# Scattering the experts' results by an exact zero-one matrix, in high and low parts, with the gate applied on VectorE

## The chip, the cores and the metric

One core of a Trainium2 chip. The metric is the device time in microseconds of one launch of the whole program; lower is better.

## The reference

Two stacked blocks over 256 tokens of width 1024. The second layer of the first block ends in a mixture of eight experts, and this is the part that the change touches. Cut to what matters:

```python
logits = (t @ w_router).astype(jnp.float32) + b_router
top_v, top_i = lax.top_k(logits, TOP_K)                     # 2 of 8
top_w = jax.nn.softmax(top_v, -1)
gates = jnp.sum(jax.nn.one_hot(top_i, N_EXPERTS) * top_w[..., None], axis=1)
out = jnp.zeros_like(t)                                     # 256 tokens x 1024
for e in range(N_EXPERTS):                                  # 3584 hidden columns each
    out = out + gates[:, e:e + 1] * _swiglu(t, wg[e], wu[e], wd[e])
x = _layer_norm(DEEPNORM_ALPHA * x + (1.0 + g_f) * out, ln_g, ln_b)
```

## The kernel before, in words

Every large matrix product is made from float32 in three products of a shorter type (fp32r in the profile): a value is split into a high part (ScalarE copies it into the shorter type, `split_hi`, line 430) and a low part (VectorE subtracts the high part from the value, `split_lo`, line 439), and TensorE adds high*high, high*low and low*high (`mm3`, lines 444 to 446). The weights stream from memory in chunks of 128x2048 values, into a ring, and the parts of a chunk lie in one of three buffers `HI` and `LO`. So ScalarE may split chunk j only when TensorE has finished chunk j-3 (`used`), VectorE takes the low part after ScalarE, and TensorE waits for the low part (`lo`).

In the expert stage each expert works on at most 128 tokens, gathered from 256. It has seven steps b (512 hidden columns each); n = 7x + b counts all steps. TensorE's order in step n is: first gate chunk g0, the four transposes of the hidden values of step n-1 (line 544), second gate chunk g1, up chunks u0 and u1, then the two down chunks d0 and d1 of step n-1, which add into PSUM banks 5 and 6 over the seven steps of an expert. Each chunk is 12 matmuls of 512 columns.

An expert's result comes out of the banks while the next expert's step b = 0 has ended on VectorE: `dve_y` (line 2087) multiplies the two banks by a row of gains and writes the float32 tile `YE`. TensorE then scatters it to the tokens in four plain float32 matmuls (`pe_scatter`, line 1908): one after g1 of each of the steps b = 1 to 4, in bank 7, with the stationary matrix `PGT` (for each place the token and its gate). VectorE adds each quarter to `X` (line 1914). `PGT` comes from `PG`, made on VectorE (`dve_select`, lines 1853 and 1854), turned by TensorE (`pe_turn`) and copied by ScalarE (line 1897). The last expert's result is scattered after the loop (`pe_last_scatter`), in four banks, and is followed on TensorE by products of another part (`pe_keys`, line 1636).

The order of the work is written out by hand, and every engine runs its own list in order. ScalarE and VectorE split three chunks ahead of the program's step: at the loop's start g0, g1 and u0 are split. So in step n ScalarE's list is: split u1, copy of the turned hidden values (line 2004), split d0, silu (2031), split d1, split g0 of the next step, split g1, split u0. VectorE's list is: split u1, low part of the hidden values (2009), split d0, scatter's addition or the select, split d1, split g0 of the next step, product of gate and up (2068), split g1, split u0, and, in step b = 0, `dve_y`.

```python
def dve_y(v, x):
    if x > 1:
        v.wait_ge(*pe_moe("scatter", x - 2, 3))
    for nb in range(2):
        ns = slice(512 * nb, 512 * nb + 512)
        v.wait_ge(*(pe_moe("lastdown") if (x, nb) == (7, 0) else used(CH[f"moe{x}d"][13])))
        z = v.tensor_tensor(YE[:, x % 2, ns], PS[:, 5 + nb, :], GB2[:, ns], ALU.mult)
```

Of the kernel before, what the change touches and what calls it, by code (L numbers as in the profile page):

```python
# [7 lines left out]
F32 = mybir.dt.float32  # L8
# [221 lines left out]
def emit_program(nc, ctx, A, out):  # L230
# [1514 lines left out]
    HM = ar(6144, 2, 1024)  # L1745
    RK, RP, RP2, GG, LGT = [ar(8192 + 16 * i, 2, 8) for i in range(5)]
    m1, den2, CNT = ar(8272, 2), ar(8274, 2), ar(8280, 8)
    PP, PG, PGT = ar(8448, 2, 2, 128), ar(8960, 2, 2, 128), ar(9472, 2, 256)
    SGm, HFm = ar(9984, 2, 512), ar(11008, 2, 512)
    YE = ar(12032, 2, 1024)  # L1750
    GB2, LG2, LB2 = ar(14080, 1024), ar(15104, 1024), CST[:, C_DEC:C_DEC + 1024]
    CMP, CM2 = ar(9984, 2, 8, 8), ar(10112, 2, 8, 8)
    SCR, SHR = ar(12032, 1024), ar(13056, 1024)
    GH = X1H[:, :, :].rearrange("p a b -> p (a b)").rearrange("p (s c n) -> p s c n", s=2, c=8)
    GL = X1L[:, :, :].rearrange("p a b -> p (a b)").rearrange("p (s c n) -> p s c n", s=2, c=8)
    RHm = X2H[:, :, :].rearrange("p a b -> p (a b)").rearrange("p (s c n) -> p s c n", s=4, c=4)
    RLm = X2L[:, :, :].rearrange("p a b -> p (a b)").rearrange("p (s c n) -> p s c n", s=4, c=4)

    def pe_router(t):
        t.wait_ge(*act_two("memory", "router"))  # L1760
# [87 lines left out]
    def dve_select(v, x):  # L1848
        s_ = x % 2
        if x > 1:  # L1850
            v.wait_ge(*pe_moe("turn", x - 2))
        for k in range(2):
            v.tensor_scalar(PP[:, s_, k, :], iota, RP[:, k, x:x + 1], None, ALU.is_equal)
            z = v.tensor_scalar(PG[:, s_, k, :], iota, RP[:, k, x:x + 1], GG[:, k, x:x + 1], ALU.is_equal, ALU.mult)
        z.then_inc(*dve_moe.up("select", x))

    def gather_bank(x, half):
# [28 lines left out]
                        gh.bitcast(F32), ALU.subtract).then_inc(*dve_moe.up("gather", x, half))  # L1886

    def pe_turn(t, x):
        if x:
            t.wait_ge(*dve_moe("gather", x, 1))  # L1890
        turn(t, [(PS[:, 7 if x else 6, 128 * k:128 * k + 128], PG[:, x % 2, k, :]) for k in range(2)]).then_inc(*pe_moe.up("turn", x))

    def act_turn(a, x):
        a.wait_ge(*pe_moe("turn", x))
        if x > 1:
            a.wait_ge(*pe_moe("scatter", x - 2, 3))
        a.activation(PGT[:, x % 2, :], PS[:, 7 if x else 6, 0:256], ACT.Copy).then_inc(*act_moe.up("turn", x))
# [4 lines left out]
    def pe_scatter(t, x, q):  # L1902
        k, ns = q // 2, slice(512 * (q % 2), 512 * (q % 2) + 512)
        if q == 0:
            t.wait_ge(*dve_moe("y", x))
        if x < 7:
            t.wait_ge(*(dve_moe("scatter", x, q - 1) if q else act_moe("turn", x + 1)))
        t.matmul(PS[:, scatter_bank(x, q), :], PGT[:, x % 2, 128 * k:128 * k + 128], YE[:, x % 2, ns], start=True,  # L1908
                 stop=True).then_inc(*pe_moe.up("scatter", x, q))

    def dve_scatter(v, x, q):
        k, ns = q // 2, slice(512 * (q % 2), 512 * (q % 2) + 512)
        v.wait_ge(*pe_moe("scatter", x, q))
        v.tensor_tensor(X[:, k, ns], X[:, k, ns], PS[:, scatter_bank(x, q), :], ALU.add).then_inc(
            *dve_moe.up("scatter", x, q))

    def pe_between(t, x, b, after):
        if x > 0 and 1 <= b <= 4 and after == "g":  # L1920
            pe_scatter(t, x - 1, b - 1)
        if x < 7 and (b, after) == (5, "u"):
            pe_gather(t, x + 1, 0)
        if x < 7 and (b, after) == (6, "g"):
            pe_gather(t, x + 1, 1)
        if x < 7 and (b, after) == (6, "u"):
            pe_turn(t, x + 1)

    def act_between(a, x, b, after):
        if x < 7 and (b, after) == (5, "u"):  # L1930
            act_gather(a, x + 1, 0)
        if x < 7 and (b, after) == (6, "g"):
            act_gather(a, x + 1, 1)
        if x < 7 and (b, after) == (6, "u"):
            act_turn(a, x + 1)

    def dve_between(v, x, b, after):
        if x > 0 and 1 <= b <= 4 and after == "g":
# [8 lines left out]
    def pe_moe_program(t):  # L1947
        pe_router(t)
        pe_gather(t, 0, 0)
        pe_gather(t, 0, 1)  # L1950
        pe_turn(t, 0)
        for n in range(7 * NEXP + 1):
            x, b = n // 7, n % 7
            for q, nm in ((0, "g"), (1, "u")) if x < NEXP else ():
                bk = 2 * q + n % 2
                for k in range(2):
                    i = CH[f"moe{x}{nm}"][2 * b + k]
                    t.wait_ge(*lo(i))
# [12 lines left out]
            if n > 0:
                pe_down(t, n - 1)

    def pe_down(t, n):
        x, b = n // 7, n % 7
        for half in range(2):
            i = CH[f"moe{x}d"][2 * b + half]
            t.wait_ge(*lo(i))
            if half == 0:
                t.wait_ge(*dve_moe("hidlo", n))  # L1980
            if x > 0 and b == 0 and half == 0:
                t.wait_ge(*dve_moe("y", x - 1))
            for nb, c in ((0, 0), (0, 1), (1, 0), (1, 1)):
                ns, q = slice(512 * nb, 512 * nb + 512), 2 * half + c
                z = mm3(t, PS[:, 5 + nb, :], RHm[:, n % 3, q, :], RLm[:, n % 3, q, :], hi_of(i)[:, c, ns],
                        lo_of(i)[:, c, ns], b == 0 and q == 0, b == 6 and q == 3)
                if n == 55 and half == 1 and (nb, c) == (0, 1):
                    z.then_inc(*pe_moe.up("lastdown"))
            z.then_inc(*used.up(i))
            if n == 54 and half == 0:  # L1990
                pe_turn_hidden(t, 55)
# [7 lines left out]

    def act_hidden_moe(a, n):  # L2000
        a.wait_ge(*pe_moe("hid", n))
        if n > 2:
            a.wait_ge(*used(CH[f"moe{(n - 3) // 7}d"][2 * ((n - 3) % 7) + 1]))
        a.activation(RHm[:, n % 3], PS[:, 4, :].rearrange("p (c n) -> p c n", c=4), ACT.Copy).then_inc(
            *act_moe.up("hid", n))

    def dve_hidden_moe(v, n):
        v.wait_ge(*act_moe("hid", n))
        v.tensor_tensor(RLm[:, n % 3], PS[:, 4, :].rearrange("p (c n) -> p c n", c=4), RHm[:, n % 3].bitcast(F32),
                        ALU.subtract).then_inc(*dve_moe.up("hidlo", n))  # L2010

    def act_moe_program(a):
# [3 lines left out]
        split_hi(a)  # L2016
        act_gather(a, 0, 0)
        act_gather(a, 0, 1)
        act_turn(a, 0)
        for n in range(7 * NEXP + 1):  # L2020
            x, b = n // 7, n % 7
            if x < NEXP:
# [56 lines left out]

    def dve_y(v, x):  # L2080

        if x > 1:
            v.wait_ge(*pe_moe("scatter", x - 2, 3))
        for nb in range(2):
            ns = slice(512 * nb, 512 * nb + 512)
            v.wait_ge(*(pe_moe("lastdown") if (x, nb) == (7, 0) else used(CH[f"moe{x}d"][13])))
            z = v.tensor_tensor(YE[:, x % 2, ns], PS[:, 5 + nb, :], GB2[:, ns], ALU.mult)
        z.then_inc(*dve_moe.up("y", x))


    def pe_last_scatter(t):
# [34 lines left out]

    XG, HT2 = ar(0, 8, 128), ar(1024, 4, 128)
    WB2 = [ar(2048, 2048), ar(4096, 2048)]
    P1, G1, GT1, Y1 = ar(8448, 2, 128), ar(8704, 2, 128), ar(8960, 256), ar(12032, 1024)
    H1 = ar(9984, 512)  # L2130

    def wb(i, c):
# [1069 lines left out]

    def vector_y(v):
        dve_y(v, 7)

    count = Count()
    for program in (sync_program, scalar_program, vector_program, gpsimd_program, tensor_program, vector_y, sp_rest,
                    act_rest_body, dve_rest_body, pe_rest_body, sync_program2, scalar_program2, vector_program2,
                    gpsimd_program2, tensor_program2):
        program(count)  # L3210
# [9 lines left out]
    with nc.Block() as blk:  # L3220
# [6 lines left out]
            tensor_program2(t)  # L3227

        def scalar_end(a):
            with a.If(more(a)):  # L3230
                act_rest_body(a)
            scalar_program2(a)

# [46 lines left out]
```

## Time and profile before

| | |
|---|---|
| three runs | 2753.72, 2753.80, 2757.09 us |
| median | 2753.8 us |
| span of the profiled execution | 2756.4 us (no other time of it is given) |
| TensorE busy in it | 2655.7 us, 96% |
| VectorE | 2194.9 us, 80% |
| ScalarE | 1519.4 us, 55% |
| GpSimd | 47.4 us, 2% |
| mean granted TensorE clock | 0.973 of full speed |
| expert stage, from its first chunk to its last | 597.4 to 1591.4 us |

Times in the rows count from the span's start. A matmul's time is from its start to its modelled end, and matmuls overlap, so what one costs is the distance between two starts, which the chain of waits gives. PE is TensorE, PEld its weight loads, DVE VectorE, ACT ScalarE, POOL GpSimd. Names such as `PS<-AR` are the tiles written and read: PS is PSUM, AR the arena in which most tiles of this stage lie.

### The profile page before, as it was taken

Reading aid. Unit: us, or ns where it says so; the run is one execution under the profiler, and the core shown is the slowest. Engines: PE = TensorE matmul, PEld = TensorE weight load, DVE = VectorE, ACT = ScalarE, POOL = GpSimd, SP = SyncE. Lnnn points to the kernel's source line nnn. Section 1 sums busy time; section 2 is a strip of 40 time slices with the busy share of each in tenths; the row PEclk is TensorE's granted clock in tenths of the full one; section 3 lists DMA queues with packets and bytes.
Section 4 is the critical chain, followed back from the end, with each engine's and each line's share of the span. In section 5 each row is a group of like instructions: output and inputs, shape, how many; then the busy total and the mean of one; then the engine's idle time right before and its main releaser. Section 6 shows DMA issues by size and latency. Waiting matters only on the chain.

```text
span 2756.4 us, 37885 instructions
## 1 busy us (share of the span) xinstructions
PE 2655.7 (96%) x15712; PEld 2358.6 (86%) x15712; DVE 2194.9 (80%) x2513; ACT 1519.4 (55%) x1567; POOL 47.4 (2%) x83
## 2 busy tenths in 40 slices
PE   6969999989999999999999999999999999999998
PEld 5859998878888888888888889999899999998898
DVE  6967677778888888888888879885487788954777
ACT  3514335547677677777777754544554564444554
POOL 2000000000000000000000000000000000000000
PEclk9979999989999999999999999999999998999999
DMA  8649865369999999999999952354455533444453
GB/s 312 235 162 336 312 240 168 120 212 378 351 350 353 345 359 349 360 348 358 348 359 346 364 184 87 135 183 173 157 184 184 186 125 130 154 153 168 153 184 115
DMA packets 376065, 669.86 MB, mean 243 GB/s; under 512 B 26825, under 2 KB 199503, under 8 KB 371023
## 3 DMA queue, kind: packets, MB, share of 16 engines
q1 hardware_dynamic: 358400, 662.55, 68.2%
q10 hardware_dynamic: 17487, 4.83, 0.7%
q8 instruction: 126, 2.06, 0.3%
q14 instruction: 52, 0.43, 0.0%
HBM read 663.13 MB, written 4.19 MB: 242 GB/s over the span
## 4 chain that ended last, share of the span: by engine, by line
PE 88%; DVE 7%; ACT 2%; DMA 1%; issue 1%; POOL 0%; ACTq 0%; SPq 0%; DVEq 0%; POOLq 0%
PE PS L444 25%; PE PS L446 24%; PE PS L445 24%; PE PS L544 2%; PE PS L2477 2%; DVE LO L439 2%; PE PS L1636 2%; DVE AR L2767 1%; PE PS L1871 1%; PE PS L1908 1%; PE PS L2363 1%; DMA RAW<-in_w_ada_dram 1%; ACT HI L430 1%; DVE AR L697 1%; PE PS L2354 1%
## 5 line engine op out<-in xcount | busy, mean ns | idle before, releaser
L439 DVE TENSOR_TENSOR LO<-RAW,HI 128x2048 fp32r<-128x2048 f32 x410 | 930.2, 2273 | 231.5 <-ACT HI L430 231.3
L430 ACT ACTIVATE HI<-RAW 128x2048 fp32r<-128x2048 f32 x410 | 780.0, 1903 | 346.3 <-PE PS L446 292.9
L444 PE MATMUL PS<-X1H,HI 128*128 128x256 f32 (+1 forms) x2128 | 611.4, 287 | 6.2 <-DVE X1L L584 4.2
L445 PE MATMUL PS<-X1L,HI 128*128 128x256 f32 (+1 forms) x2128 | 605.5, 285 | 0.0
L446 PE MATMUL PS<-X1H,LO 128*128 128x256 f32 (+1 forms) x2128 | 605.2, 284 | 0.0
L444 PE MATMUL PS<-HI,X1H 128*128 128x512 f32 x1056 | 431.6, 409 | 0.9 <-DVE LO L439 0.4
L444 PEld LDWEIGHTS PS<-X1H,HI 128*128 128x128 f32 (+1 forms) x2128 | 409.4, 192 | 11.1 <-issue 8.5
L446 PE MATMUL PS<-HI,X1L 128*128 128x512 f32 x1056 | 413.7, 392 | 0.0
L445 PE MATMUL PS<-LO,X1H 128*128 128x512 f32 x1056 | 413.0, 391 | 0.0
L445 PEld LDWEIGHTS PS<-X1L,HI 128*128 128x128 f32 (+1 forms) x2128 | 409.6, 192 | 2.0
L446 PEld LDWEIGHTS PS<-X1H,LO 128*128 128x128 f32 (+1 forms) x2128 | 409.3, 192 | 0.8
L439 DVE TENSOR_TENSOR LO<-AR,HI 128x2048 fp32r<-128x2048 f32 (+1 forms) x147 | 334.8, 2278 | 58.6 <-ACT HI L430 57.7
L430 ACT ACTIVATE HI<-AR 128x2048 fp32r<-128x2048 f32 (+1 forms) x147 | 280.2, 1907 | 121.3 <-PE PS L446 117.0
L444 PE MATMUL PS<-HI,X2H 128*128 128x512 f32 x840 | 333.9, 398 | 3.3 <-DVE LO L439 3.3
L445 PE MATMUL PS<-LO,X2H 128*128 128x512 f32 x840 | 330.8, 394 | 0.0
L446 PE MATMUL PS<-HI,X2L 128*128 128x512 f32 x840 | 330.5, 393 | 0.0
L444 PEld LDWEIGHTS PS<-HI,X1H 128*128 128x128 f32 x1056 | 199.2, 189 | 48.3 <-issue 8.5
L445 PEld LDWEIGHTS PS<-LO,X1H 128*128 128x128 f32 x1056 | 199.4, 189 | 45.5 <-issue 6.7
L446 PEld LDWEIGHTS PS<-HI,X1L 128*128 128x128 f32 x1056 | 198.8, 188 | 42.9
L2767 DVE SCALAR_TENSOR_TENSOR AR<-AR,PC 128x256 f32<-128x256 f32 x480 | 193.9, 477 | 0.1
L444 PEld LDWEIGHTS PS<-HI,X2H 128*128 128x128 f32 x840 | 160.4, 191 | 35.7 <-DVE LO L439 3.7
L446 PEld LDWEIGHTS PS<-HI,X2L 128*128 128x128 f32 x840 | 159.8, 190 | 34.1
(392 smaller groups left out, 2869.0 us busy)
## 6 DMA issues: line engine op xcount, KB each, us to landing
RAW<-in_w_in_dram SPq DMA_DIRECT2D x66, 1024.0 KB, 5.2
RAW<-in_expert_w_gate_dram SPq DMA_DIRECT2D x66, 1024.0 KB, 5.2
RAW<-in_expert_w_up_dram SPq DMA_DIRECT2D x64, 1024.0 KB, 5.2
RAW<-in_expert_w_down_dram SPq DMA_DIRECT2D x62, 1024.0 KB, 5.3
RAW<-in_ffn_w_up_dram SPq DMA_DIRECT2D x55, 1024.0 KB, 5.6
AR<-in_expert_w_down_dram SPq DMA_DIRECT2D x50, 1024.0 KB, 5.3
AR<-in_expert_w_up_dram SPq DMA_DIRECT2D x48, 1024.0 KB, 5.5
AR<-in_expert_w_gate_dram SPq DMA_DIRECT2D x46, 1024.0 KB, 5.2
```

Of the source, the lines that this page charges most:

```text
L430: a.activation(HI[:, n % NH, 0:size(i)], raw_at(i), ACT.Copy).then_inc(*hi.up(i))
L439: v.tensor_tensor(LO[:, m % NH, 0:n], raw_at(i), HI[:, m % NH, 0:n].bitcast(F32), ALU.subtract).then_inc(*lo.up(i))
L444: t.matmul(o, lh, rh, start=first, stop=False)
L445: t.matmul(o, lh, rl, start=False, stop=False)
L446: return t.matmul(o, ll, rh, start=False, stop=last)
L544: z = t.transpose(d, s_, ident[0:n, 0:n])
L697: v.scalar_tensor_tensor(o, slot, pcol("c", k), o, ALU.mult, ALU.add).then_inc(*dve_ada.up("step", m))
L1636: z = t.matmul(PS[:, bank, 256 * nb:256 * nb + 256], w[:, c, 128 * nb:128 * nb + 128], cols[:, c, :], start=(c == 0), stop=(c == 7))
L1871: z = t.matmul(PS[:, gather_bank(x, half), 128 * c:128 * c + 128], HM[:, k, 512 * half + 128 * c:512 * half + 128 * c + 128], PP[:, x % 2, ...
L1908: t.matmul(PS[:, scatter_bank(x, q), :], PGT[:, x % 2, 128 * k:128 * k + 128], YE[:, x % 2, ns], start=True, stop=True).then_inc(*pe_moe.u ...
L2477: z = t.matmul(PS[:, b, 256 * k:256 * k + 256], MF[:, c, 128 * k:128 * k + 128], w[:, c, :], start=(c == 0), stop=(c == 7))
L2767: v.scalar_tensor_tensor(UC[:, c, :], UP[:, c, k:k + 256], pcol(f"cv_dw_w{l}", 8 * k + c), UC[:, c, :], ALU.mult, ALU.add).then_inc(*dve_t ...
```

## The change

The select now makes only the zero-one matrix `PP`, which is turned itself (for expert x instead of x+1, in the same place of the order; that of expert 7 is new there, and that of expert 0 ahead of the loop is gone) and copied into a tile `PPT` of its own. `YE` is split like a weight chunk: ScalarE copies it into `YH` (`act_y`), VectorE subtracts (`dve_y_lo`) into `YL`. The scatter is two fp32r matmuls a quarter. VectorE's addition multiplies by the gate. `YE`, `PPT`, `YH` and `YL` are single; the hidden values' parts have two buffers instead of three. The diff, cut:

```diff
-    YE = ar(12032, 2, 1024)
+    YE = ar(12032, 1024)
-    RHm = X2H[:, :, :].rearrange("p a b -> p (a b)").rearrange("p (s c n) -> p s c n", s=4, c=4)
+    RHm = X2H[:, 0:4, :].rearrange("p a b -> p (a b)").rearrange("p (s c n) -> p s c n", s=2, c=4)
+    YH, YL = [t_[:, 4:8, :].rearrange("p a b -> p (a b)") for t_ in (X2H, X2L)]
...
         for k in range(2):
-            v.tensor_scalar(PP[:, s_, k, :], iota, RP[:, k, x:x + 1], None, ALU.is_equal)
-            z = v.tensor_scalar(PG[:, s_, k, :], iota, RP[:, k, x:x + 1], GG[:, k, x:x + 1], ALU.is_equal, ALU.mult)
+            z = v.tensor_scalar(PP[:, s_, k, :], iota, RP[:, k, x:x + 1], None, ALU.is_equal)
...
     def pe_turn(t, x):
-        if x:
-            t.wait_ge(*dve_moe("gather", x, 1))
-        turn(t, [(PS[:, 7 if x else 6, 128 * k:128 * k + 128], PG[:, x % 2, k, :]) for k in range(2)]).then_inc(*pe_moe.up("turn", x))
+        t.wait_ge(*(dve_moe("gather", x + 1, 1) if x < 7 else dve_moe("scatter", 6, 3)))
+        turn(t, [(PS[:, 7, 128 * k:128 * k + 128], PP[:, x % 2, k, :]) for k in range(2)]).then_inc(*pe_moe.up("turn", x))
...
         if q == 0:
-            t.wait_ge(*dve_moe("y", x))
-        if x < 7:
-            t.wait_ge(*(dve_moe("scatter", x, q - 1) if q else act_moe("turn", x + 1)))
-        t.matmul(PS[:, scatter_bank(x, q), :], PGT[:, x % 2, 128 * k:128 * k + 128], YE[:, x % 2, ns], start=True,
-                 stop=True).then_inc(*pe_moe.up("scatter", x, q))
+            t.wait_ge(*dve_moe("ylo", x))
+            t.wait_ge(*act_moe("turn", x))
+        elif x < 7:
+            t.wait_ge(*dve_moe("scatter", x, q - 1))
+        places = PPT[:, 128 * k:128 * k + 128]
+        t.matmul(PS[:, scatter_bank(x, q), :], places, YH[:, ns], start=True, stop=False)
+        t.matmul(PS[:, scatter_bank(x, q), :], places, YL[:, ns], start=False, stop=True).then_inc(
+            *pe_moe.up("scatter", x, q))
...
-        v.tensor_tensor(X[:, k, ns], X[:, k, ns], PS[:, scatter_bank(x, q), :], ALU.add).then_inc(
-            *dve_moe.up("scatter", x, q))
+        v.scalar_tensor_tensor(X[:, k, ns], PS[:, scatter_bank(x, q), :], GG[:, k, x:x + 1], X[:, k, ns], ALU.mult,
+                               ALU.add).then_inc(*dve_moe.up("scatter", x, q))
...
     def act_hidden_moe(a, n):
         a.wait_ge(*pe_moe("hid", n))
-        if n > 2:
-            a.wait_ge(*used(CH[f"moe{(n - 3) // 7}d"][2 * ((n - 3) % 7) + 1]))
+        if n > 1:
+            a.wait_ge(*used(CH[f"moe{(n - 2) // 7}d"][2 * ((n - 2) % 7) + 1]))
...
             if 0 < n < 56:                                     # act_moe_program, end of step n
                 split_hi(a)
                 split_hi(a)
+                if b == 0:
+                    act_y(a, x - 1)
...
             if x < NEXP:                                       # dve_moe_program, start of step n
                 split_lo(v)
+                if x > 0 and b == 1:
+                    dve_y_lo(v, x - 1)
...
+    def act_y(a, x):
+        a.wait_ge(*dve_moe("y", x))
+        a.activation(YH, YE, ACT.Copy).then_inc(*act_moe.up("yhi", x))
+
+    def dve_y_lo(v, x):
+        v.wait_ge(*act_moe("yhi", x))
+        v.tensor_tensor(YL, YE, YH.bitcast(F32), ALU.subtract).then_inc(*dve_moe.up("ylo", x))
```

For the last expert `act_y` runs on ScalarE and `dve_y_lo` on VectorE at the start of the block that follows the loop, ahead of `pe_last_scatter`.

## Rows read from the trace of the kernel before

**Rows 1.** the page: busy shares, and the granted clock (tenths) in 40 slices

```profile
PE 2655.7 (96%) x15712; PEld 2358.6 (86%) x15712; DVE 2194.9 (80%) x2513; ACT 1519.4 (55%) x1567; POOL 47.4 (2%) x83
...
PEclk9979999989999999999999999999999998999999
```

**Rows 2.** busy us (and instructions) in the expert stage, one stretch per expert; PEclk is granted clock

```profile
core 0: us, PE busy (x) PEld busy (x) DVE busy (x) ACT busy (x) POOL busy (x), PEclk, DMA share, GB/s
...
722.00:846.00 124.00, 124.00 (x571) 101.68 (x570) 108.83 (x68) 87.56 (x58) 0.00 (x0) 1.00 0.97 352
```

**Rows 3.** chain of waits in the stage, start and us of each link, in order

```profile
735.96 0.23 PE PS L446
736.19 0.86 PE PS L1908 x2
```

**Rows 4.** TensorE in order of time, around expert 0's first scatter

```profile
736.03 1.02 PE L1908 MATMUL PS<-AR 128*128 128x512 f32 x2
```

**Rows 5.** VectorE in order of time, at the same border

```profile
732.32 2.29 DVE L439 TENSOR_TENSOR LO<-AR,HI 128x2048 fp32r<-128x2048 f32 x1 [0.34 <-ACT HI L430]
734.53 1.28 DVE L2087 TENSOR_TENSOR AR<-PS,AR 128x512 f32<-128x512 f32 x2
735.73 2.28 DVE L439 TENSOR_TENSOR LO<-RAW,HI 128x2048 fp32r<-128x2048 f32 x1
...
740.73 0.68 DVE L1914 TENSOR_TENSOR X<-X,PS 128x512 f32<-128x512 f32 x1
```

**Rows 6.** ScalarE in order of time, at the same border

```profile
730.37 1.92 ACT L430 ACTIVATE HI<-AR 128x2048 fp32r<-128x2048 f32 x1 [0.80 <-PE PS L446]
733.09 1.92 ACT L430 ACTIVATE HI<-RAW 128x2048 fp32r<-128x2048 f32 x1 [0.80 <-PE PS L446]
```

**Rows 7.** groups of instructions by line and shape, ScalarE: count, busy us, mean ns

```profile
L430 ACT ACTIVATE HI<-RAW 128x1024 fp32r<-128x1024 f32 x4 | 4.2, 1050 | 0.0
```

**Rows 8.** the same for VectorE

```profile
L439 DVE TENSOR_TENSOR LO<-RAW,HI 128x1024 fp32r<-128x1024 f32 x4 | 4.9, 1223 | 1.5 <-ACT HI L430 1.5
...
L2112 DVE SCALAR_TENSOR_TENSOR X<-X,SM,AR 128x512 f32<-128x512 f32 x4 | 2.8, 750 | 0.1
```

**Rows 9.** two TensorE gaps elsewhere, in stretches (columns as rows 2)

```profile
168.50:171.80 3.30, 0.06 (x1) 0.00 (x0) 3.08 (x2) 0.00 (x0) 0.00 (x0) 1.00 0.72 217
...
172.90:176.30 3.40, 3.40 (x10) 2.62 (x9) 1.78 (x2) 0.00 (x0) 0.00 (x0) 0.50 0.49 161
...
2552.00:2555.40 3.40, 0.03 (x1) 0.00 (x0) 1.31 (x3) 2.12 (x8) 1.03 (x3) 1.00 0.92 305
...
2556.40:2562.20 5.80, 5.74 (x27) 5.74 (x28) 4.24 (x11) 4.54 (x9) 0.11 (x1) 0.50 0.00 0
```

**Rows 10.** chain of waits at the stage's end

```profile
1591.39 0.70 DVE AR L2087
...
1592.37 3.70 PE PS L1908 x8
1596.08 6.92 PE PS L1636 x32
```

**Rows 11.** ScalarE's work just ahead of it

```profile
1587.84 3.29 ACT L1624 ACTIVATE RAW<-RAW,PC 128x256 f32<-128x256 f32 x8
```

**Rows 12.** VectorE in order of time, the first select

```profile
590.13 0.28 DVE L1853 TENSOR_SCALAR AR<-CST,AR 128x128 f32<-128x128 f32 x1
590.33 0.34 DVE L1854 TENSOR_SCALAR AR<-CST,AR 128x128 f32<-128x128 f32 x1
...
590.78 0.34 DVE L1854 TENSOR_SCALAR AR<-CST,AR 128x128 f32<-128x128 f32 x1
```

**Rows 13.** TensorE ahead of the stage's first chunk, in order of time

```profile
591.17 6.21 PE L1871 MATMUL PS<-AR 128*128 128x128 f32 x32 [2.85 <-DVE AR L1854]
597.22 0.38 PE L544 MATMUL PS<-CST,AR 128*128 128x128 f32 x2
597.36 0.48 PE L444 MATMUL PS<-HI,X1H 128*128 128x512 f32 x1
```

More of the change, by code:

```diff
@@ L252, in emit_program @@
     WR = sb("WR", [128, 8, 8])
+    PPT = sb("PPT", [128, 256], F32R)
     PS = ctx.enter_context(nc.psum_tensor("PS", [128, 8, 512], F32))
@@ L1747, in emit_program @@
     m1, den2, CNT = ar(8272, 2), ar(8274, 2), ar(8280, 8)
-    PP, PG, PGT = ar(8448, 2, 2, 128), ar(8960, 2, 2, 128), ar(9472, 2, 256)
+    PP = ar(8448, 2, 2, 128)
     SGm, HFm = ar(9984, 2, 512), ar(11008, 2, 512)
-    YE = ar(12032, 2, 1024)
+    YE = ar(12032, 1024)
     GB2, LG2, LB2 = ar(14080, 1024), ar(15104, 1024), CST[:, C_DEC:C_DEC + 1024]
@@ L1755, in emit_program @@
     GL = X1L[:, :, :].rearrange("p a b -> p (a b)").rearrange("p (s c n) -> p s c n", s=2, c=8)
-    RHm = X2H[:, :, :].rearrange("p a b -> p (a b)").rearrange("p (s c n) -> p s c n", s=4, c=4)
-    RLm = X2L[:, :, :].rearrange("p a b -> p (a b)").rearrange("p (s c n) -> p s c n", s=4, c=4)
+    RHm = X2H[:, 0:4, :].rearrange("p a b -> p (a b)").rearrange("p (s c n) -> p s c n", s=2, c=4)
+    RLm = X2L[:, 0:4, :].rearrange("p a b -> p (a b)").rearrange("p (s c n) -> p s c n", s=2, c=4)
+    YH, YL = [t_[:, 4:8, :].rearrange("p a b -> p (a b)") for t_ in (X2H, X2L)]
     def pe_router(t):
@@ L1888, in pe_turn @@
     def pe_turn(t, x):
-        if x:
-            t.wait_ge(*dve_moe("gather", x, 1))
-        turn(t, [(PS[:, 7 if x else 6, 128 * k:128 * k + 128], PG[:, x % 2, k, :]) for k in range(2)]).then_inc(*pe_moe.up("turn", x))
+        t.wait_ge(*(dve_moe("gather", x + 1, 1) if x < 7 else dve_moe("scatter", 6, 3)))
+        turn(t, [(PS[:, 7, 128 * k:128 * k + 128], PP[:, x % 2, k, :]) for k in range(2)]).then_inc(*pe_moe.up("turn", x))
     def act_turn(a, x):
         a.wait_ge(*pe_moe("turn", x))
-        if x > 1:
-            a.wait_ge(*pe_moe("scatter", x - 2, 3))
-        a.activation(PGT[:, x % 2, :], PS[:, 7 if x else 6, 0:256], ACT.Copy).then_inc(*act_moe.up("turn", x))
+        if x > 0:
+            a.wait_ge(*pe_moe("scatter", x - 1, 3))
+        a.activation(PPT[:, :], PS[:, 7, 0:256], ACT.Copy).then_inc(*act_moe.up("turn", x))
     def scatter_bank(x, q):
@@ L1925, in pe_between @@
             pe_gather(t, x + 1, 1)
-        if x < 7 and (b, after) == (6, "u"):
-            pe_turn(t, x + 1)
+        if (b, after) == (6, "u"):
+            pe_turn(t, x)
     def act_between(a, x, b, after):
@@ L1933, in act_between @@
             act_gather(a, x + 1, 1)
-        if x < 7 and (b, after) == (6, "u"):
-            act_turn(a, x + 1)
+        if (b, after) == (6, "u"):
+            act_turn(a, x)
     def dve_between(v, x, b, after):
@@ L1950, in pe_moe_program @@
         pe_gather(t, 0, 1)
-        pe_turn(t, 0)
         for n in range(7 * NEXP + 1):
@@ L1984, in pe_down @@
                 ns, q = slice(512 * nb, 512 * nb + 512), 2 * half + c
-                z = mm3(t, PS[:, 5 + nb, :], RHm[:, n % 3, q, :], RLm[:, n % 3, q, :], hi_of(i)[:, c, ns],
+                z = mm3(t, PS[:, 5 + nb, :], RHm[:, n % 2, q, :], RLm[:, n % 2, q, :], hi_of(i)[:, c, ns],
                         lo_of(i)[:, c, ns], b == 0 and q == 0, b == 6 and q == 3)
@@ L2001, in act_hidden_moe @@
         a.wait_ge(*pe_moe("hid", n))
-        if n > 2:
-            a.wait_ge(*used(CH[f"moe{(n - 3) // 7}d"][2 * ((n - 3) % 7) + 1]))
-        a.activation(RHm[:, n % 3], PS[:, 4, :].rearrange("p (c n) -> p c n", c=4), ACT.Copy).then_inc(
+        if n > 1:
+            a.wait_ge(*used(CH[f"moe{(n - 2) // 7}d"][2 * ((n - 2) % 7) + 1]))
+        a.activation(RHm[:, n % 2], PS[:, 4, :].rearrange("p (c n) -> p c n", c=4), ACT.Copy).then_inc(
             *act_moe.up("hid", n))
@@ L2008, in dve_hidden_moe @@
         v.wait_ge(*act_moe("hid", n))
-        v.tensor_tensor(RLm[:, n % 3], PS[:, 4, :].rearrange("p (c n) -> p c n", c=4), RHm[:, n % 3].bitcast(F32),
+        v.tensor_tensor(RLm[:, n % 2], PS[:, 4, :].rearrange("p (c n) -> p c n", c=4), RHm[:, n % 2].bitcast(F32),
                         ALU.subtract).then_inc(*dve_moe.up("hidlo", n))
@@ L2018, in act_moe_program @@
         act_gather(a, 0, 1)
-        act_turn(a, 0)
         for n in range(7 * NEXP + 1):
@@ L2080, in dve_y @@
     def dve_y(v, x):
-        if x > 1:
-            v.wait_ge(*pe_moe("scatter", x - 2, 3))
+        if x > 0:
+            v.wait_ge(*pe_moe("scatter", x - 1, 3))
         for nb in range(2):
@@ L2086, in dve_y @@
             v.wait_ge(*(pe_moe("lastdown") if (x, nb) == (7, 0) else used(CH[f"moe{x}d"][13])))
-            z = v.tensor_tensor(YE[:, x % 2, ns], PS[:, 5 + nb, :], GB2[:, ns], ALU.mult)
+            z = v.tensor_tensor(YE[:, ns], PS[:, 5 + nb, :], GB2[:, ns], ALU.mult)
         z.then_inc(*dve_moe.up("y", x))
+    def act_y(a, x):
[4 more added lines that the diff above has]
+        v.tensor_tensor(YL, YE, YH.bitcast(F32), ALU.subtract).then_inc(*dve_moe.up("ylo", x))
     def pe_last_scatter(t):
@@ L2128, in emit_program @@
     WB2 = [ar(2048, 2048), ar(4096, 2048)]
-    P1, G1, GT1, Y1 = ar(8448, 2, 128), ar(8704, 2, 128), ar(8960, 256), ar(12032, 1024)
+    P1, G1, GT1, Y1 = ar(8448, 2, 128), ar(8704, 2, 128), ar(8960, 256), ar(11008, 1024)
     H1 = ar(9984, 512)
@@ L3204, in vector_y, with scalar_y @@
         dve_y(v, 7)
+        dve_y_lo(v, 7)
+    def scalar_y(a):
+        act_y(a, 7)
     count = Count()
-    for program in (sync_program, scalar_program, vector_program, gpsimd_program, tensor_program, vector_y, sp_rest,
+    for program in (sync_program, scalar_program, vector_program, gpsimd_program, tensor_program, vector_y, scalar_y, sp_rest,
                     act_rest_body, dve_rest_body, pe_rest_body, sync_program2, scalar_program2, vector_program2,
@@ L3229, in scalar_end @@
         def scalar_end(a):
-            with a.If(more(a)):
+            flag = more(a)
+            scalar_y(a)
+            with a.If(flag):
                 act_rest_body(a)
```

## The prediction

> **What bounds the kernel now.** The page comes first [rows 1]: TensorE is busy for 96% of the span, at full granted clock nearly throughout. The stage that the change touches lies at 597 to 1591 us, and the stretches by expert show what it is bound by [rows 2]: in the 124.00 us of one expert TensorE is busy for 124.00, at clock 1.00, with VectorE at 108.8 and ScalarE at 87.6. So a matmul removed there is time removed, and a wait of TensorE put there is time added, one for one. The chain of waits in the stage [rows 3] is TensorE alone and gives true prices: an fp32r matmul of 512 columns is 0.23 us (twelve of them, a chunk, 2.72 us by the starts of the chunks), and one float32 quarter of the scatter, which runs as two passes, is 0.86 us. The next thing to see is how little room the scatter has. At the border between experts 0 and 1 TensorE begins it at 736.03 [rows 4], while VectorE ends `YE` at 734.53 + 1.28 = 735.81 [rows 5]: 0.22 us ahead. The other borders that I looked at are the same to 0.01 us. `YE` can't come sooner as the lists stand: it stands behind the low part of u0 (732.32), which began when ScalarE's high part ended (730.37 + 1.92), which began when TensorE gave the buffer free [rows 5, 6].
>
> **The change, part by part.** All against the profiled execution, whose span of 2756.4 us lies 2.6 above the median of 2753.8; I carry the differences to the median, since the work is the same.
>
> *The matmuls of the scatter.* In the loop seven experts have four quarters: 28 times 0.86 become 28 times 2 x 0.227 (0.454), so 28 x 0.41 = 11.4 us go [rows 3]. All on the path.
>
> *The split of the result, and who waits.* This is the large term, so I replay one border on the lists. `YE` is ready at 735.81. ScalarE has done its high part of u0 at 732.29 and now stands at `act_y`, as the next entry of its list is behind it. It starts at 735.85. A high part of 128x1024 takes 1.05 us [rows 7]: to 736.90. Only then comes the high part of u1, which before ran at 733.09 [rows 6]; now it runs from 736.81 (ScalarE's operations overlap by 0.09) to 738.73. VectorE's list has the low part of u1 ahead of `dve_y_lo`: before at 735.73, now 738.76, and the next operation starts 2.21 later, at 740.97. The low part of 128x1024 takes 1.22 us [rows 8]: to 742.19. TensorE's scatter, due at 736.03, waits for it until 742.24, so 6.2 us, and since TensorE runs its list in order, u0 (whose parts have long been ready) stands behind it, and every later chunk with it. In the meantime the others get ahead: u1 is ready at 741.0, and d0 follows at about 745.0 against its need at 748, so nothing is late next. Buffers of the hidden values: two are enough, since the products that used a buffer are on TensorE's list ahead of the transposes that refill it: 0 us. 7 borders x 6.2 = 43.4 us. Bounds: if u1's split were not late, `YE`'s two parts would still take 1.05 + 1.22, so at least 2.1 us a border (14.7); if ScalarE's copy took as long as a full one (1.92, rows 6), 7.1 us (49.7). The rows of just these shapes decide for 6.2.
>
> *The clock after the wait.* No gap of 6 us is in this stage, but elsewhere gaps show what follows [rows 9]. After a gap of 3.3 us the granted clock was 0.50 (the lower level, 1.2 GHz) for 3.4 us of work. After one of 4.4 us it was 0.50 in the 5.8 us of work that followed. At the lower level work takes twice as long, so half of that is lost: 1.7 or 2.9 us. For the low end I set 0, as gaps of 1 us at the end of this stage cost nothing. I take 1.7 for each of the seven, the nearer end because the longer the gap, the more of the slow stretch falls into the gap itself: 11.9 us, bounds 0 and 20.3. The Trainium skill ("TensorE: Matmul & The Clock Gate", on HAM oscillation) says that repeated waits of TensorE make its array fall back to the slow clock each time; by that rule each border pays, and the rows above say the same, with the sizes used here. Were the rule not to hold in this stage, the sum would be 11.9 us less.
>
> *VectorE and ScalarE otherwise.* The select loses two of four operations and `dve_y_lo` is one more; in the stage VectorE idles 15 us an expert [rows 2], and ahead of the select's next split it waits for ScalarE anyway: 0. The addition with the gate is a three-operand form: 0.75 against 0.68 us [rows 8, 5], hidden by the same idle time; if that cover were gone, 28 x 0.07 = 2 us. ScalarE's copy of the turned matrix is where it was: 0.
>
> *The front.* The gather waits for the first select [rows 13], whose four operations start at 590.13, 590.33, then the other pair, the last at 590.78 and 0.34 long [rows 12]. With two left it ends 0.5 us sooner. The two transposes ahead of the loop go (597.22 to 597.36, 0.14). Together -0.6 us. Expert 7's two transposes are new inside the loop, for the same 0.14: +0.1.
>
> *The end.* Before: second half of `YE` 1591.39 to 1592.09, scatter at 1592.37, next products at 1595.91 to 1596.08 [rows 10]. After: ScalarE is free by 1591.13 [rows 11], so 1592.13 + 1.05 + 1.22 and the 0.28 to TensorE, that is 1594.7, or 1594.9 if ScalarE too needs 0.28 in the new block. Eight fp32r matmuls take 1.8 (the eight float32 passes took 3.6), so the next products start at 1596.6, +0.7 us. VectorE's chain of norms starts 2.0 later, but ScalarE's squares, which need it, come late enough behind TensorE's products to take up nearly all of it: 0, at most 1.2 (both are covered by the bounds). TensorE's gap of 3.5 us is like the 3.3 in [rows 9]: +1.7. Together +2.4, bounds 0.6 and 3.6.
>
> **Sum:** -11.4 + 43.4 + 11.9 - 0.6 + 0.1 + 2.4 = +45.8 us. 2753.8 + 45.8 = 2799.6, said as 2800.
>
> **The rivals.**
> 1. *The split comes in time, and only the matmuls count* (faster). The place is the wait of the first quarter: with the two parts of the result ready within 0.2 us, 28 x 0.41 and the front are gained, -11.9, and the end gives back 2.4: 2744. It decides from a loss of 1.4 us a border on ((11.4 + 0.6 - 0.1 - 2.4) / 7); below that the kernel is faster. For it: ScalarE is busy for only 71% of an expert. Against: the lists; its free time lies elsewhere than where the copy stands, and even with no list in the way 1.05 + 1.22 us don't fit in 0.2. Chance 0.04.
> 2. *The waits come, the clock stays up.* 2800 - 11.9 - 1.7 = 2786. For it: the page's row of the clock is at 9 tenths or full in nearly all slices, though there are waits in many [rows 1]. Against: [rows 9], where the clock fell after both gaps. Chance 0.12.
> 3. *Every gap costs like the longer row, or the scatter in parts saves nothing* (if the program were to run it in the passes of before). The first: 2800 + 7 x 1.2 + 1.2 = 2810; the second: 2800 + 11.4 = 2811. For the first: 6.2 us is nearer to 4.4 than to 3.3. Against the second: operands of this type run at 0.23 us in [rows 3]. Chance 0.2.
> 4. *The wait is shorter*, with 2 to 5 us a border, by something in the lists that I misread: 2753.8 + 7 x 3.5 - 11.4 + 7 x 0.85 + 2.4 = 2775. Chance 0.06.
>
> **How the numbers follow.** The forecast itself has 0.58. A measurement of this kernel tells about 0.2% (5.5 us) from no change. Slower by more than that are the forecast, rivals 2, 3 and 4: 0.94 with a little off for what I haven't seen; faster is rival 1. The range runs from 2783, just under rival 2, to 2814, over both forms of rival 3; rivals 1 and 4 and some unknown are outside.
>
> **What would show it.** In the changed trace TensorE's first scatter matmul of each of seven experts has idle time of about 6 us ahead of it, released by VectorE's subtraction of 128x1024; ScalarE idles 3.5 us ahead of the 128x1024 copy; u1's low part starts 3 us later than before against `YE`. The clock in the stage's slices is no longer 1.00, with half-rate stretches behind each of the gaps. Scatter matmuls stand 0.23 us apart. TensorE's share in an expert falls below 96%. I am wrong if the gap is missing or below 2 us, or if the low half is ready when TensorE comes.

## The result, and the profile after

The changed kernel takes 2806.2 us (median of four runs, 2805.47 to 2809.61) against 2753.76 for the kernel before on the same chip: a ratio of 1.019, with a 95% interval of 1.0177 to 1.0204. It is slower by 52.4 us. The profiled execution took 2806.1 us, with a span of 2804.3.

The page, to be read beside [rows 1]: TensorE does the same number of matmuls, but its share is 95%, and in the row of the clock one slice more reads 8. That one lies behind the stage; the stage's own slices of 70 us still read 9 tenths or more, so the clock has to be looked at closer, below.

```profile
PE 2661.3 (95%) x15712; PEld 2369.8 (85%) x15712; DVE 2204.0 (79%) x2505; ACT 1526.3 (54%) x1575; POOL 47.4 (2%) x83
...
PEclk9979999989999999999999999899999998999999
```

TensorE's list at the first border, in order of time. It answers to [rows 4]: the wait of the first scatter matmul is new, and the matmuls behind it (L445 is the first of each chunk's triples) stand 1.28 us apart in threes, not 0.68.

```profile
731.67 0.39 PE L445 MATMUL PS<-HI,X1H 128*128 128x512 f32 x1
...
738.54 0.80 PE L1910 MATMUL PS<-X2H,PPT 128*128 128x512 f32 x1 [6.03 <-DVE X2L L2101]
739.14 0.63 PE L1911 MATMUL PS<-X2L,PPT 128*128 128x512 f32 x1
739.57 0.63 PE L445 MATMUL PS<-HI,X1H 128*128 128x512 f32 x1
...
740.85 0.63 PE L445 MATMUL PS<-HI,X1H 128*128 128x512 f32 x1
...
742.12 0.63 PE L445 MATMUL PS<-HI,X1H 128*128 128x512 f32 x1
...
743.32 0.39 PE L445 MATMUL PS<-HI,X1H 128*128 128x512 f32 x1
...
744.02 0.39 PE L445 MATMUL PS<-HI,X1H 128*128 128x512 f32 x1
```

VectorE's and then ScalarE's list at the same place, answering to [rows 5, 6].

```profile
728.65 2.29 DVE L440 TENSOR_TENSOR LO<-AR,HI 128x2048 fp32r<-128x2048 f32 x1 [0.35 <-ACT HI L431]
730.86 1.28 DVE L2092 TENSOR_TENSOR AR<-PS,AR 128x512 f32<-128x512 f32 x2
735.06 2.29 DVE L440 TENSOR_TENSOR LO<-RAW,HI 128x2048 fp32r<-128x2048 f32 x1 [2.92 <-ACT HI L431]
737.27 1.22 DVE L2101 TENSOR_TENSOR X2L<-AR,X2H 128x1024 fp32r<-128x1024 f32 x1
```

```profile
732.17 1.06 ACT L2097 ACTIVATE X2H<-AR 128x1024 fp32r<-128x1024 f32 x1 [3.56 <-DVE AR L2092]
733.14 1.89 ACT L431 ACTIVATE HI<-RAW 128x2048 fp32r<-128x2048 f32 x1
```

The reader is to see a chain with no free moment in it: result ready at 730.86 + 1.28 = 732.14, copy of 1.06 us from 732.17 (ScalarE had waited 3.56 us for it), u1's high part at 733.14, its low part at 735.06 (VectorE had waited 2.92 us), the result's low part at 737.27 to 738.49, scatter at 738.54. TensorE idled for 6.03 us. The seven borders are alike: 6.03 or 6.04 us each.

The same places by stretches (columns: length, then busy us and instructions of TensorE, its weight loads, VectorE, ScalarE and GpSimd, then the granted clock). Each pair is a gap and what follows it, at the first three borders; the last line is what follows the 3.13 us gap at the stage's end.

```profile
732.50:738.50 6.00, 0.01 (x1) 0.00 (x0) 3.44 (x3) 5.30 (x5) 0.00 (x0) 0.82 0.57 197
738.50:743.20 4.70, 4.66 (x11) 3.69 (x12) 3.45 (x3) 0.00 (x0) 0.00 (x0) 0.50 0.79 241
...
864.50:870.50 6.00, 0.01 (x1) 0.00 (x0) 3.44 (x3) 5.29 (x5) 0.00 (x0) 0.92 0.58 201
870.50:876.30 5.80, 5.76 (x14) 4.51 (x15) 3.44 (x3) 0.00 (x0) 0.00 (x0) 0.50 0.82 269
996.90:1003.00 6.10, 0.09 (x1) 0.00 (x0) 3.46 (x3) 5.38 (x5) 0.00 (x0) 0.69 0.58 203
1003.00:1006.00 3.00, 2.97 (x7) 2.39 (x8) 3.00 (x3) 0.00 (x0) 0.00 (x0) 0.50 0.93 328
...
1639.00:1643.00 4.00, 4.00 (x18) 3.40 (x19) 3.11 (x6) 0.00 (x0) 0.06 (x1) 1.00 0.06 18
```

The lower level (1.2 GHz) is granted for 4.7, 5.8 and 3.0 us of work here, and over the seven borders for 32.3 us. A matmul is started every 0.43 us there and every 0.23 us at the upper level, so about half of that time is lost, 16.2 us. At the stage's end it is not granted in this execution.

### The profile page after: what moved, and what is told of

The parts are those of the page before. It is cut to its first block, busy times and chain, and to the rows that moved or that the text cites. A ratio compares the mean times of both kernels' runs of the same rounds, so it can differ in the third digit from the quotient of the medians.

```text
span 2804.3 us, 37889 instructions
## 1 busy us (share of the span) xinstructions
PE 2661.3 (95%) x15712; PEld 2369.8 (85%) x15712; DVE 2204.0 (79%) x2505; ACT 1526.3 (54%) x1575; POOL 47.4 (2%) x83
## 4 chain that ended last, share of the span: by engine, by line
PE 87%; DVE 8%; ACT 2%; DMA 2%; issue 1%; POOL 0%; ACTq 0%; SPq 0%; DVEq 0%; POOLq 0%
PE PS L445 25%; PE PS L446 24%; PE PS L447 24%; PE PS L545 2%; DVE LO L440 2%; PE PS L2490 2%; PE PS L1637 1%; ACT HI L431 1%; DVE AR L2780 1%; PE PS L1872 1%; PE PS L2376 1%; DMA RAW<-in_w_ada_dram 1%; PE PS L2367 1%; DVE AR L698 1%; PE PS L726 1%
## 5 line engine op out<-in xcount | busy, mean ns | idle before, releaser
L445 PE MATMUL PS<-X1H,HI 128*128 128x256 f32 (+1 forms) x2128 | 611.4, 287 | 6.0 <-DVE X1L L585 4.2
L445 PE MATMUL PS<-HI,X1H 128*128 128x512 f32 x1056 | 425.4, 403 | 0.9 <-DVE LO L440 0.4
L445 PEld LDWEIGHTS PS<-X1H,HI 128*128 128x128 f32 (+1 forms) x2128 | 409.8, 193 | 10.8 <-issue 8.3
L445 PE MATMUL PS<-HI,X2H 128*128 128x512 f32 x840 | 333.0, 396 | 2.7 <-DVE LO L440 2.7
L445 PEld LDWEIGHTS PS<-HI,X1H 128*128 128x128 f32 x1056 | 202.6, 192 | 44.4 <-issue 1.8
L445 PEld LDWEIGHTS PS<-HI,X2H 128*128 128x128 f32 x840 | 159.9, 190 | 35.0 <-DVE LO L440 3.1
```

What stands on the lines that cost most here:

```text
L445: t.matmul(o, lh, rh, start=first, stop=False)
```

## The experiments

Each was compared with runs of the kernel before on its own chip, whose median was 2755.7 us for e1 to e4 and 2757.3 for e6 to e8; so ratios, not bare times, are compared between groups. There is also a finer measure, which leaves out everything around the stage: the period of an expert, from one run of 16 gather matmuls (at the end of a step b = 6) to the next, taken over six experts of the profiled execution.

**e1, the scatter one step later.** The split stays where the change has it.

```diff
-        if x > 0 and 1 <= b <= 4 and after == "g":
-            pe_scatter(t, x - 1, b - 1)
+        if x > 0 and 2 <= b <= 5 and after == "g":
+            pe_scatter(t, x - 1, b - 2)
```

and the same for VectorE's additions.

> The changed kernel with its four scatter quarters one step later (steps 2 to 5 of the next expert, on TensorE and VectorE); the split of the result stays where it is. Theory A (a wait made by the order of the lists): the 6.03 us wait ahead of the scatter goes, but the high part of u1 still stands behind the copy of the result on ScalarE, so TensorE waits about 2.2 us a border for u1's low part (ready at 741.0 on the clock of the kernel before, wanted at 738.75). 2806.2 - 7 x 3.8 = 2779 if the clock still falls after each of these shorter gaps, 2763 if it doesn't. Theory B (ScalarE and VectorE are short of time for the added copy and subtraction, whatever their place): the same work, so within 5 us of 2806.

Measured: 2771.42 us, ratio 1.0055 (1.004 to 1.007). TensorE's waits in the stage, first the list, then two stretches after gaps:

```profile
PE PS L445 <- DVE LO L440: 18.0, 10, 2.2
```

```profile
740.11 0.50 PE L445 MATMUL PS<-HI,X1H 128*128 128x512 f32 x1 [2.19 <-DVE LO L440]
...
744.04 0.50 PE L445 MATMUL PS<-HI,X2H 128*128 128x512 f32 x1 [0.92 <-DVE LO L440]
```

```profile
740.10:744.00 3.90, 3.01 (x12) 2.18 (x12) 3.90 (x4) 2.98 (x3) 0.00 (x0) 1.00 0.73 237
...
868.80:872.20 3.40, 3.40 (x9) 2.47 (x8) 3.40 (x3) 1.24 (x2) 0.00 (x0) 0.50 0.72 286
```

The wait for the result's parts is gone, and the second one that the first had hidden stands in the open: u1's low part comes 2.19 us late, as expected. After the first such gap the clock stayed up (and a second gap of 0.92 us followed); after the second it fell for 3.4 us. It fell after four of the seven, and the gap of 0.9 us came only behind the three after which it stayed up. So the time lies between the two that theory A gave (2763 and 2779), and theory B, by which the place doesn't matter, is out.

**e2, the split where the engines are free.** Same instructions, other places on the lists: ScalarE copies the result after u1's high part and the copy of the hidden values, VectorE subtracts after d0's low part, and TensorE scatters after u1 instead of after g1.

```diff
-        if x > 0 and 1 <= b <= 4 and after == "g":
+        if x > 0 and 1 <= b <= 4 and after == "u":
             pe_scatter(t, x - 1, b - 1)
...
-        if x > 0 and 1 <= b <= 4 and after == "g":
+        if x > 0 and b == 1 and after == "g":
+            dve_y_lo(v, x - 1)
+        if x > 0 and 1 <= b <= 4 and after == "u":
             dve_scatter(v, x - 1, b - 1)
...
             if 0 < n < 56:
                 act_hidden_moe(a, n - 1)
+                if x > 0 and b == 1:
+                    act_y(a, x - 1)
...
                 split_hi(a)
                 split_hi(a)
-                if b == 0:
-                    act_y(a, x - 1)
...
                 split_lo(v)
-                if x > 0 and b == 1:
-                    dve_y_lo(v, x - 1)
```

> The same instructions as the changed kernel in another order: ScalarE copies the result after u1's high part and the copy of the hidden values, VectorE subtracts after d0's low part, TensorE scatters after u1 of the steps 1 to 4 instead of after g1. Theory A: no wait of TensorE at the borders, granted clock 1.00 through the stage; what is left is the gain on the matmuls, 28 x 0.41 = 11.4 us, and about +0.5 at the end: 2743, faster than both kernels. Theory B: the waits move but stay, total above 2780.

Measured: 2751.97 us (12 runs, 2744.57 to 2756.21), ratio 0.9985 (0.9975 to 0.9995). The waits moved and shrank to a tenth, but were not gone:

```profile
735.00 0.39 PE L447 MATMUL PS<-HI,X1L 128*128 128x512 f32 x1
735.99 0.50 PE L1910 MATMUL PS<-X2H,PPT 128*128 128x512 f32 x1 [0.60 <-DVE X2L L2101]
736.33 0.39 PE L1911 MATMUL PS<-X2L,PPT 128*128 128x512 f32 x1
```

```profile
732.51 2.29 DVE L440 TENSOR_TENSOR LO<-RAW,HI 128x2048 fp32r<-128x2048 f32 x1
734.72 1.22 DVE L2101 TENSOR_TENSOR X2L<-AR,X2H 128x1024 fp32r<-128x1024 f32 x1
```

I had put the subtraction behind d0's low part (732.51), which ends late, and TensorE came 0.6 us too soon; from start to start that is 0.99 instead of 0.23, so 0.76 x 7 = 5.3 us. The clock stayed at 1.00 through the stage. So the same copy and subtraction that made TensorE wait 6.2 us a border in one place cost 0.8 in another, though here the scatter stands 2.7 us later too. Against the 11 us expected the gain is 4.1 by the ratio (1.4 to 6.9), and the stage of the profiled execution is 4.7 us shorter than before; the seven waits are most of what is missing.

**e3, matmuls in the wait.**

```diff
         if q == 0:
+            t.wait_ge(*act_moe("turn", x))
+            if x < 7:
+                for r in range(24):
+                    t.matmul(PS[:, 7, :], GH[:, (x + 1) % 2, r % 8, :], GL[:, (x + 1) % 2, 0:4, :], start=True, stop=True)
             t.wait_ge(*dve_moe("ylo", x))
-            t.wait_ge(*act_moe("turn", x))
```

> The changed kernel with 24 added fp32r matmuls of 512 columns (24 x 0.227 = 5.4 us, on tiles that are ready, into bank 7 ahead of the scatter, which writes over them) in each of the seven waits. The wait itself is thereby kept, only TensorE is busy in it. Theory A (16 us of the loss are the half-rate stretches behind the gaps): clock 1.00 through the stage, 2806.2 - 16.2 = 2790. Rival C (the slow stretches are covered by waits for ScalarE and VectorE, or would be there anyway): 2806, within 3 us.

Measured: 2790.16 us, ratio 1.0122 (1.0108 to 1.0137), against 1.019 of the changed kernel. 168 matmuls more, and 16 us less by the medians, 19 by the ratios.

```profile
732.23 5.60 PE L1908 MATMUL PS<-X1L,X1H 128*128 128x512 f32 x24
738.43 0.50 PE L1913 MATMUL PS<-X2H,PPT 128*128 128x512 f32 x1 [0.60 <-DVE X2L L2104]
...
739.00 0.40 PE L445 MATMUL PS<-HI,X1H 128*128 128x512 f32 x1
...
739.69 0.39 PE L445 MATMUL PS<-HI,X1H 128*128 128x512 f32 x1
```

```profile
600.00:1570.00 970.00, 965.79 (x4464) 799.58 (x4463) 828.69 (x498) 672.66 (x452) 0.00 (x0) 1.00 0.95 343
```

The wait itself is as long as ever (from 732.23 to 738.43), but behind it the triples stand 0.69 us apart at once, and the granted clock of the stage is 1.00. In the profiled executions the stage, from its first gather matmul to the last chunk's end, takes 1048.3 us in the changed kernel and 1033.3 here. So 15.1 of the 16.2 us that I put down to the clock went with it; about 1 us isn't accounted for. The total alone would not say this so closely, since parts outside the stage differ too: at the stage's end the clock fell here, which it had not in the changed kernel, and that piece took 3.7 us longer.

**e4, the gate alone.** The result is not split, so copy and subtraction are gone; one float32 matmul a quarter.

```diff
-    PPT = sb("PPT", [128, 256], F32R)
+    PPT = sb("PPT", [128, 256])
...
-            t.wait_ge(*dve_moe("ylo", x))
+            t.wait_ge(*dve_moe("y", x))
...
-        t.matmul(PS[:, scatter_bank(x, q), :], places, YH[:, ns], start=True, stop=False)
-        t.matmul(PS[:, scatter_bank(x, q), :], places, YL[:, ns], start=False, stop=True).then_inc(
+        t.matmul(PS[:, scatter_bank(x, q), :], places, YE[:, ns], start=True, stop=True).then_inc(
```

> Only one part of the change: the zero-one matrix, turned late and copied as float32, one float32 matmul a quarter, the gate applied in VectorE's addition; the result is not split (no copy, no subtraction), single result tile, two buffers of hidden values. Theory A (the split alone costs): 2753.8 - 0.5, so the kernel before within 2 us. Rival D (a part of the loss comes from the three-operand addition, the single tiles or the two buffers): above 2756, up to 2760.

Measured: 2752.87 us (11 runs), ratio 0.9995 (0.9984 to 1.0006): no change. The gate in the addition, the single tiles, the two buffers and the later turn cost nothing that can be told; the interval leaves room for 1.7 us. The stage took 1000.0 us, against 1000.2 before.

**e6, split as in e2, scatter as in e1.** It takes e2's split and puts the quarters after g1 of steps 2 to 5; these lines are against e2.

```diff
-        if x > 0 and 1 <= b <= 4 and after == "u":
-            pe_scatter(t, x - 1, b - 1)
+        if x > 0 and 2 <= b <= 5 and after == "g":
+            pe_scatter(t, x - 1, b - 2)
```

> e2 with the scatter's quarters after g1 of steps 2 to 5 instead of after u1 of steps 1 to 4, so 2.7 us later against the split. In e2 TensorE still waited 0.76 us a border for the low part. Theory A: those seven waits go (-5.3 us against e2), nothing in the stage is waited for, and the stage is shorter than before by the matmuls, about 11 us; the total is 9 to 12 us under the kernel before of the same chip. Rival (e2 missed its expected gain for another reason, such as dearer chunks beside the added work): the same total as e2, 4 us under the kernel before.

Measured: 2746.96 us, ratio 0.9966 (0.9953 to 0.998), so 9 to 10 us under the kernel before (5 to 13 by the interval), where 9 to 12 were expected. In the stage no scatter matmul waits. One small wait stays, of weight loads for a low part (d1's, at each border), so the stage is 8.5 us shorter than before, and not 11:

```profile
PEld PS L445 <- DVE LO L440: 3.9, 8, 0.5
```

e6 and e1 are the clean pair for the place of the split: the instructions are the same and the scatter stands in the same place, only copy and subtraction have moved. The ratio falls from 1.0055 to 0.9966, and the stage from 1016.9 to 991.6 us.

**e7, the last result by halves.** For the last expert copy, subtraction and the first two quarters' waits go by 512 columns. This is ScalarE's part of the edit, on top of e6:

```diff
+        if x == 7:
+            a.wait_ge(*dve_moe("yfirst"))
+            a.activation(YH[:, 0:512], YE[:, 0:512], ACT.Copy).then_inc(*act_moe.up("yhifirst"))
+            a.wait_ge(*dve_moe("y", x))
+            a.activation(YH[:, 512:1024], YE[:, 512:1024], ACT.Copy).then_inc(*act_moe.up("yhi", x))
+            return
```

> e6 with the last expert's result split by halves of 512 columns, so that TensorE's first quarter after the loop waits for half of the copy and half of the subtraction. The gap of TensorE there, 3.13 us in the changed kernel, falls by about 1.3 us to 1.8, and so does the time against e6: 1 to 1.5 us less. If the end isn't bound by this chain, nothing changes.

Measured: 2744.8 us, ratio 0.9958 (0.9943 to 0.9974). Against e6 that is 2.2 us less, but the two intervals overlap, so by the totals alone it isn't shown. The lists at the stage's end show it, e6 first, then e7:

```profile
1578.92 0.80 PE L1910 MATMUL PS<-X2H,PPT 128*128 128x512 f32 x1 [3.13 <-DVE X2L L2101]
...
1597.33 1.94 PE L545 MATMUL PS<-CST,AR 128*128 128x128 f32 x16 [1.04 <-DVE AR L2311]
```

```profile
1582.34 0.50 PE L1913 MATMUL PS<-X2H,PPT 128*128 128x512 f32 x1 [1.38 <-ACT X2H L2105]
...
1599.65 1.94 PE L545 MATMUL PS<-CST,AR 128*128 128x128 f32 x16 [1.04 <-DVE AR L2328]
```

The gap is 1.38 instead of 3.13 us, a little better than the 1.8 expected. (The profile names ScalarE's second copy as what ended it; the program waits there for VectorE's first half, which ended at 1582.29.) From the scatter to the next transposes it is 17.3 instead of 18.4; in e6 the clock fell after the gap and in e7 it did not. Of the versions that add both parts this one has the lowest median, and it is faster than both kernels.

**e8, the matmuls by themselves.** VectorE writes the result in the shorter type at once, and both matmuls of a quarter use it: the low part is left out and the high part is added twice. The sums that it makes are not the reference's; it is there for its time alone.

```diff
-            z = v.tensor_tensor(YE[:, ns], PS[:, 5 + nb, :], GB2[:, ns], ALU.mult)
+            z = v.tensor_tensor(YH[:, ns], PS[:, 5 + nb, :], GB2[:, ns], ALU.mult)
...
-        t.matmul(PS[:, scatter_bank(x, q), :], places, YL[:, ns], start=False, stop=True).then_inc(
+        t.matmul(PS[:, scatter_bank(x, q), :], places, YH[:, ns], start=False, stop=True).then_inc(
```

> The price of the matmuls by themselves: VectorE writes the result straight in the shorter type and both matmuls of a quarter use it (the low part is left out, and the high part is added twice), so there is no copy, no subtraction and no wait for them. Theory A: 28 x 0.41 = 11.4 us in the loop and 1.5 at the end less than before, no gap at the borders: 2741 against 2753.8. If the shorter type saves nothing in this place: 2753.

Measured: 2742.23 us, ratio 0.9942 (0.9923 to 0.9962), 15.1 us less, where 12.8 were expected; in the profiled executions the stage is 11.1 us shorter and its end 1.5. The period of an expert is the cleanest measure. Here is the first of them in the kernel before, e8 and e6, in this order (one line is the run at the end of expert 0, the next that of expert 1):

```profile
700.36 1.95 PE L1871 MATMUL PS<-AR 128*128 128x128 f32 x16
```

```profile
825.48 1.95 PE L1871 MATMUL PS<-AR 128*128 128x128 f32 x16
```

```profile
697.72 1.95 PE L1872 MATMUL PS<-AR 128*128 128x128 f32 x16
```

```profile
821.24 1.95 PE L1872 MATMUL PS<-AR 128*128 128x128 f32 x16
```

```profile
692.91 1.95 PE L1872 MATMUL PS<-AR 128*128 128x128 f32 x16
```

```profile
816.85 1.95 PE L1872 MATMUL PS<-AR 128*128 128x128 f32 x16
```

That is 125.12, 123.52 and 123.94 us. Taken over six periods it is 125.12, 123.51 and 123.92: the matmuls save 1.61 us an expert, four times 0.40, and e6 gives 0.4 of it back by the small wait above. The changed kernel's period is 131.93 us and e2's 124.37. So against e8, which has no split, copy and subtraction cost 8.4 us a border where the change puts them, 0.9 in e2 and 0.4 in e6.

## Why the prediction was right, and where a term was off

*The direction and the total.* +52.4 against +45.8 forecast, 2806.2 within 2783 to 2814. The total alone would speak for the third rival as well (2810 or 2811); it is the rows and the experiments that decide. And it is in part luck that it came so near: the clock at the borders was put 4.3 us too low and the end 1.9 too high.

*The rivals.* The first (split in time) and the fourth (a wait of 2 to 5 us) fell with the gap of 6.03 us, the second with the clock at the borders; the third's price for the clock, 2.9 us each, was too high as mine was too low, and its other form fell with e8's saving.

*The wait.* The replay gave a scatter at 742.24 when it was due at 736.03, 6.2 us. Measured from the end of the last matmul the gap is 6.03, and from the time at which the scatter was due 6.2. Each link is as worked out: ScalarE's copy 1.06 (1.05), its wait for it 3.56 (3.5), low part 1.22. e1 shows both halves of the argument, and e6 against e1 that the place of the split makes the wait, and not the work in it.

*The matmuls.* 11.4 us forecast for seven experts; e8 gives 7 x 1.61 = 11.3. At the stage's end, where the clock stayed up, the scatter's matmuls stand 0.23 us apart, as forecast.

*The clock.* This is the mis-sized term. I took 1.7 us a border, on the ground that a longer gap hides more of the slow stretch. The rows at the borders show 4.67, 5.79, 3.01, 4.92, 5.92, 3.06 and 4.95 us of work at the lower level, so 2.3 us each, 16.2 in all and not 11.9. The argument was wrong in one point: the longer gap also brought a slow stretch of 6.83 us at all seven, twice the 3.4 that followed the 3.3 us gap of [rows 9], so more was left of it. The other gap of [rows 9], of 4.4 us, already had 5.8 us of slow work behind it, more than the shorter one and not less. e3 confirms the size but for 1 us. The Trainium skill ("TensorE: Matmul & The Clock Gate", on HAM oscillation) tells of a kernel whose repeated waits of about 3 to 5 us drop the array to its slow clock each time; seven of seven gaps of 6.03 us agree with it. e1's gaps of 2.2 us are shorter than those waits, and there the clock still fell at four of seven.

*The front.* The wait of the first gather fell from 2.85 to 2.35 us, the 0.5 forecast. The 0.1 for the two transposes is not seen: from the first gather matmul to the first chunk it is 6.19 us before and 6.21 after.

*The end.* Forecast +2.4, of which 1.7 was the clock. From the last chunk's end to the next part's transposes the profiled execution took 19.57 us before (1591.35 to 1610.92) and 20.11 after (1635.85 to 1655.96): +0.5, near the 0.7 without the clock. In e6 the clock did fall there, and the piece took 21.5 us.

*The gate, the buffers, the select:* 0 forecast, and e4 measures none.

*What the sum leaves open.* Stage: 43.3 (seven waits of 6.19, start to start) + 16.2 - 11.3 = 48.2; the trace has 48.15, from the first gather matmul to the last chunk's end (1000.18 us before, 1048.33 after). With the end 48.7. The spans of the two profiled executions differ by 47.9 and the medians by 52.4. The pieces of each span show where: ahead of the stage, the stage, and what follows its end (the end itself is told above; columns as above), first before and then after:

```profile
0.00:591.10 591.10, 516.93 (x3260) 465.24 (x3260) 443.56 (x586) 237.16 (x320) 27.83 (x41) 0.91 0.65 226
591.10:1591.30 1000.20, 1000.13 (x4584) 821.63 (x4584) 872.31 (x537) 709.19 (x479) 0.00 (x0) 1.00 0.98 354
...
1610.90:2756.40 1145.50, 1121.09 (x7796) 1058.15 (x7796) 866.08 (x1371) 567.52 (x757) 15.04 (x35) 0.98 0.47 158
```

```profile
0.00:587.50 587.50, 514.47 (x3260) 463.27 (x3260) 443.47 (x584) 237.31 (x320) 27.84 (x41) 0.92 0.66 227
587.50:1635.80 1048.30, 1006.04 (x4584) 832.01 (x4584) 879.67 (x529) 714.94 (x486) 0.00 (x0) 0.97 0.93 338
...
1655.90:2804.20 1148.30, 1124.84 (x7796) 1060.97 (x7796) 866.42 (x1371) 567.48 (x757) 15.04 (x35) 0.98 0.47 158
```

Ahead of the stage the changed kernel took 3.6 us less, of which the select explains 0.5, and behind it 2.8 us more, with the same program there. In both pieces the lower clock was granted for different times: ahead of the stage for 105.8 us in all before and 99.0 after, behind it for 10.2 us in its longest stretch before and 13.7 after.

```profile
1705.40:1716.00 10.60, 10.60 (x46) 10.12 (x46) 9.88 (x28) 3.00 (x4) 0.00 (x0) 0.52 0.00 0
```

```profile
1750.00:1764.00 14.00, 14.00 (x58) 13.16 (x58) 12.67 (x40) 3.22 (x5) 0.00 (x0) 0.51 0.00 0
```

That last stretch is no mark of the change: it lasted 10.2 us in e1 to e4 as well and 13.7 in e6 to e8. The profiled execution of the kernel before was itself slower than its median by about 4.4 us (its time is its span and the 1.8 us that all other executions here have beside theirs; an estimate), and that is the step from 47.9 to 52.4. So 48.7 us are traced to the change, and the 3.7 to the medians' difference are not; the interval of the ratio reaches from 48.7 to 56.2 us, and runs of the kernel before alone reach from 2749.1 to 2761.5.

## What to carry to other kernels

When an engine runs a list in order, the cost of a new step is read from what stands behind it on the list and who waits for that, not from the engine's idle share: the same copy and subtraction cost 8.4 us a border in one place (6.2 of waiting and 2.3 of clock, by the rows), 0.9 in another and 0.4 in a third, where the scatter stands later too. Moving the scatter alone (e1) was not enough. Put a new producer after the work whose consumer comes soonest, and its consumer one step later if there is room. And price a repeated wait of TensorE with the slow stretch that follows it.

## What was not expected of the hardware

After a gap of 6.03 us the lower clock was granted for 6.83 us each time, but it began anywhere from 2.2 to 5.1 us after the gap's start, so between 3.0 and 5.9 us of it fell on work. After gaps of 2.18 us it was granted four times of seven, for 3.41 us. After the gap of 3.13 to 3.22 us at the stage's end it stayed up in the changed kernel and fell in e1, e2, e3 and e6. So after gaps of 2 to 3 us the clock fell in some cases and stayed up in others, at the same place of the program. And 24 matmuls whose result nobody reads, put in each wait, made the stage 15.1 us shorter.
